# Rotary embedding moved into the projection's PSUM slot, with the statistics factor folded into its tables

## The reference

```python
def rms_norm(x, g):
    y = xf * lax.rsqrt(jnp.mean(xf * xf, axis=-1, keepdims=True) + NORM_EPS)
    return (y * g.astype(jnp.float32)).astype(x.dtype)

def partial_rope(x, cos, sin):
    x1, x2 = x[..., :half], x[..., half:2 * half]
    return concatenate([x1 * c - x2 * s, x2 * c + x1 * s, x[..., 2 * half:]], axis=-1)

h = rms_norm(x, norm_g)
q, k, v, gate = jnp.split(h @ w_in, 4, axis=-1)
q = partial_rope(q.reshape(B, L, 2 * A_HEADS, A_HEAD_DIM), cos, sin)
k = partial_rope(k.reshape(B, L, 2 * A_HEADS, A_HEAD_DIM), cos, sin)
...
w = p[:, :, 0] - lam * p[:, :, 1]          # two softmaxes of one head
```

## Time and profile before

| | us |
|---|---|
| Median of three runs | 3052.21 |
| The profiled execution | 3053.24 |
| Its span (first to last instruction) | 3051.5 |
| PE busy | 2915.2 |
| DVE busy | 1403.8 |
| POOL busy | 1225.6 |
| ACT busy | 979.3 |

### The profile page before, as it was taken

How to read it: one execution, slowest core, us unless ns; L and a number is a source line. 1 busy time by engine, 2 the same in 40 slices (tenths; PEclk the granted TensorE clock), 3 DMA queues, 4 the chain that set the end, 5 groups by cost and what they waited for, 6 DMA issues and landing times.

```text
span 3051.5 us, 41339 instructions
## 1 busy us (share of the span) xinstructions
PE 2915.2 (96%) x16960; PEld 2473.9 (81%) x16960; DVE 1403.8 (46%) x2243; ACT 979.3 (32%) x1440; POOL 1225.6 (40%) x888
## 2 busy tenths in 40 slices
PE   7999999999999988999999997999999999999976
PEld 7999999999899987777878786777777777777754
DVE  6443443434443448454444457432323334463556
ACT  4313222222313244334142434432232322333332
POOL 4343433434343423442534354544434343344331
PEclk9999999999999999999999998999999999999999
DMA  4121212222121212121212232322222222221211
GB/s 168 61 92 70 83 70 84 71 83 83 56 97 69 84 63 69 70 83 70 85 68 97 70 117 86 108 80 86 83 69 90 76 83 76 77 87 69 83 56 69
DMA packets 36944, 247.45 MB, mean 81 GB/s; under 512 B 3970, under 2 KB 4115, under 8 KB 8212
## 3 DMA queue, kind: packets, MB, share of 16 engines
q1 hardware_dynamic: 35728, 241.36, 22.4%
q10 hardware_dynamic: 1028, 3.44, 0.3%
HBM read 240.59 MB, written 4.19 MB: 80 GB/s over the span
## 4 chain that ended last, share of the span: by engine, by line
PE 85%; DVE 9%; ACT 2%; DVEq 2%; issue 1%; DMA 0%; ACTq 0%; POOL 0%; SPq 0%
PE pj L288 19%; PE pj L292 18%; PE pj L294 18%; PE pj L319 4%; PE pj L323 4%; PE pj L321 4%; PE pj L973 2%; PE pj L974 2%; PE pj L975 2%; DVE xl L366 2%; DVE arena L412 2%; PE pa L510 1%; PE pa L472 1%; PE pa L904 1%; DVEq L414 1%
## 5 line engine op out<-in xcount | busy, mean ns | idle before, releaser
L2041 POOL TENSOR_TENSOR wl<-raw,wh 128x512 fp32r<-128x512 f32 x884 | 1225.4, 1418 | 1790.6 <-ACT wh L264 1790.6
L288 PE MATMUL pj<-xh,wh 128*128 128x264 f32 (+2 forms) x3792 | 1112.6, 340 | 22.0 <-POOL wl L2041 17.7
L292 PE MATMUL pj<-xl,wh 128*128 128x264 f32 (+2 forms) x3792 | 1079.5, 331 | 13.4 <-DVE xl L366 13.3
L294 PE MATMUL pj<-xh,wl 128*128 128x264 f32 (+2 forms) x3792 | 1074.7, 330 | 0.0
L264 ACT ACTIVATE wh<-raw 128x2048 fp32r<-128x2048 f32 x221 | 423.0, 1914 | 1056.0 <-PE pj L294 647.7
L288 PEld LDWEIGHTS pj<-xh,wh 128*128 128x128 f32 x3792 | 651.1, 191 | 108.3 <-issue 41.1
L292 PEld LDWEIGHTS pj<-xl,wh 128*128 128x128 f32 x3792 | 648.9, 190 | 87.3 <-DVE xl L366 21.3
L294 PEld LDWEIGHTS pj<-xh,wl 128*128 128x128 f32 x3792 | 650.1, 191 | 64.8
L337 DVE TENSOR_TENSOR arena<-pj,rstd 128x512 f32<-128x512 f32 (+1 forms) x151 | 105.4, 698 | 399.1 <-PE pj L294 387.6
L319 PE MATMUL pj<-oh,wh 128*128 128x264 f32 (+1 forms) x800 | 222.7, 330 | 14.9 <-DVE ol L739 11.4
L345 DVE TENSOR_TENSOR acc<-pj,acc 128x528 f32<-128x528 f32 (+1 forms) x224 | 156.5, 699 | 143.4 <-PE pj L323 142.5
(11 more groups left out here) (276 smaller groups left out, 2657.2 us busy)
## 6 DMA issues: line engine op xcount, KB each, us to landing
raw<-in_stream SPq DMA_DIRECT2D x221, 1024.0 KB, 4.8
acc<-in_x SPq DMA_DIRECT2D x8, 528.0 KB, 9.2
out_y<-acc SPq DMA_DIRECT2D x8, 512.0 KB, 2.9
arena<-in_mem ACTq DMA_DIRECT2D x2, 1024.0 KB, 6.3
cst<-in_cst SPq DMA_DIRECT2D x1, 448.0 KB, 13.5
cos<-in_cos_a SPq DMA_DIRECT2D x1, 264.0 KB, 13.7
sin<-in_sin_a SPq DMA_DIRECT2D x1, 264.0 KB, 13.9
cos<-in_cos_b ACTq DMA_DIRECT2D x1, 264.0 KB, 2.8
```

The source lines that it names most:

```text
L288: pe.matmul(pj[:, pu, b, 0:m], whk, xh[:, k, a:a + m], start=(k == 0), stop=False)
L292: pe.matmul(pj[:, pu, b, 0:m], whk, xl[:, k, a:a + m], start=False, stop=False)
L294: ins = pe.matmul(pj[:, pu, b, 0:m], wlk, xh[:, k, a:a + m], start=False, stop=(k == KD - 1))
L2041: pool.tensor_tensor(wl[:, j, at], raw[:, j, at], wh[:, j, at].bitcast(F32), ALU.subtract).then_inc(s_part if c < LO_PARTS - 1 else s_lo, 1)
```

## The change

The statistics factor is multiplied into both tables once per layer (`fold_rstd`, two DVE instructions over 128 partitions). The rotary step reads the projection's PSUM slot: the product with the cosine table goes to SBUF, then the slot's rotated rows are shuffled in place (two instructions, one for each bank of 264), multiplied by the sine table in place, and added to the SBUF rows. The slot is handed back to PE after the last of these. For query 0 of the next head the shuffle goes from the slot to `tmp`, the slot is handed back after it, and one product with the sine table stands before add 4; the other steps inside `add_out` are gone. On PE the scores of units 0 and 1 stand ahead of k steps 5 and 8 instead of 3 and 7.

```diff
-            proj(pe, t + 2, u + 2, 0, 0, T, hooks={3: [a_scores(h, 0)], 7: [a_scores(h, 1)], 10: [a_scores(h, 2)],
+            proj(pe, t + 2, u + 2, 0, 0, T, hooks={5: [a_scores(h, 0)], 8: [a_scores(h, 1)], 10: [a_scores(h, 2)],
                                                    12: [a_wtr(h, 0, 0)], 15: [a_scores(h, 3)]})
-        def rope(dve, x, n, rows, mask):
-
-            dve.stream_shuffle(tmp[0:rows, 0:n], x[0:rows, 0:n], mask)
-            dve.drain()
-            dve.tensor_tensor(tmp[0:rows, 0:n], tmp[0:rows, 0:n], sin[0:rows, 0:n], ALU.mult)
-            dve.tensor_tensor(x[0:rows, 0:n], x[0:rows, 0:n], cos[0:rows, 0:n], ALU.mult)
-            dve.drain()
-            return dve.tensor_tensor(x[0:rows, 0:n], x[0:rows, 0:n], tmp[0:rows, 0:n], ALU.add)
...
+        def fold_rstd(dve, n):
+
+            for table in (cos, sin):
+                dve.tensor_tensor(table[:, 0:n], table[:, 0:n], rstd[:, 0:n], ALU.mult)
+            dve.drain()
+
+        def rope(dve, x, u, pu, n, rows, mask, view=None):
+
+            view = (lambda ap: tok(ap, n)) if view is None else view
+            ps = ps_out(pu, n)
+            dve.wait_ge(s_out, u + 2)
+            dve.tensor_tensor(x, view(ps) if n != T else ps, view(cos[:, 0:n]), ALU.mult)
+            dve.drain()
+            for b, at, m in halves(n):
+                half = pj[0:rows, pu, b, 0:m]
+                dve.stream_shuffle(half, half, mask)
+            dve.drain()
+            dve.tensor_tensor(ps[0:rows], ps[0:rows], tok(sin[0:rows, 0:n], n), ALU.mult)
+            dve.drain()
+            ins = dve.tensor_tensor(x[0:rows], view(ps[0:rows]) if n != T else ps[0:rows], x[0:rows], ALU.add)
+            dve.drain()
+            dve.sem_inc(s_evac, 1)
+            return ins
...
-            evac_scaled(dve, A_q[0], u + 1, 1, T).then_inc(s_evac, 1)
-            dve.drain()
-            steps = rope_steps(dve, A_q[0], T, A_ROT, A_MASK)
...
-                add_out(dve, w, T, 0, between={4: steps[0], 7: steps[1], 10: steps[2]})
...
+                dve.wait_ge(s_out, u + 3)
+                dve.tensor_tensor(tok(A_q[0], T), ps_out(1, T), tok(cos[:, :], T), ALU.mult)
+                for b, at, m in halves(T):
+                    dve.stream_shuffle(tmp[0:A_ROT, at:at + m], pj[0:A_ROT, 1, b, 0:m], A_MASK)
+                dve.drain()
+                dve.sem_inc(s_evac, 1)
+                x, y = A_q[0][0:A_ROT, :], tmp[0:A_ROT, :]
+                add_out(dve, w, T, 0, between={4: lambda: dve.tensor_tensor(y, y, sin[0:A_ROT, :], ALU.mult)})
+                dve.tensor_tensor(x, x, y, ALU.add)
+                dve.drain()
...
             dve.wait_ge(s_tab, 32)
+            fold_rstd(dve, T)
             for c in range(2):
-                evac_scaled(dve, B_x, U_KV + c, c, T).then_inc(s_evac, 1)
-                dve.drain()
-                rope(dve, B_x, T, P, B_MASK)
-                dve.drain()
+                rope(dve, tok(B_x, T), U_KV + c, c, T, P, B_MASK)
...
+            rope(dve, B_q[:, :, m, :], u, pu, SEQ, P, B_MASK, view=b_tok)
+            dve.sem_inc(s_bq, 1)
```

More of the change, by code:

```diff
@@ L646, in a_first @@
         def a_first(dve, u, w=None):
-            evac_scaled(dve, A_k[0], u, 0, T).then_inc(s_evac, 1)
-            dve.drain()
-            rope(dve, A_k[0], T, A_ROT, A_MASK).then_inc(s_rope, 1)
-            dve.drain()
-            evac_scaled(dve, A_q[0], u + 1, 1, T).then_inc(s_evac, 1)
-            dve.drain()
-            steps = rope_steps(dve, A_q[0], T, A_ROT, A_MASK)
+            rope(dve, tok(A_k[0], T), u, 0, T, A_ROT, A_MASK)
+            dve.sem_inc(s_rope, 1)
             if w is None:
-                for f in steps:
-                    f()
-            else:
-                add_out(dve, w, T, 0, between={4: steps[0], 7: steps[1], 10: steps[2]})
-            dve.drain()
-            dve.tensor_tensor(A_q[0][0:A_ROT, :], A_q[0][0:A_ROT, :], tmp[0:A_ROT, :], ALU.add).then_inc(s_rope, 1)
-            dve.drain()
+                rope(dve, tok(A_q[0], T), u + 1, 1, T, A_ROT, A_MASK)
+            else:
+                dve.wait_ge(s_out, u + 3)
[8 more added lines that the diff above has]
+                dve.drain()
+            dve.sem_inc(s_rope, 1)
         def a_dve(dve, h, last=False):
@@ L666, in a_dve @@
             for j, x in enumerate([A_k[1], A_q[1]]):
[L667 to L670, removed]
+                rope(dve, tok(x, T), u + j, j, T, A_ROT, A_MASK)
+                dve.sem_inc(s_rope, 1)
             for j in (2, 3, 4):
```

## The result

The changed kernel takes 3035.67 us (median of 5 runs, 3035.24 to 3041.51) beside 3052.28 of the kernel before in the same comparison: ratio 0.9945, 95% interval 0.9931 to 0.996, so 12 to 21 us faster. In a second comparison it was 3038.19 beside 3055.42, ratio 0.9946 (0.9933 to 0.996). The profiled execution took 3035.24 us, its span is 3033.5, against 3053.24 and 3051.5 before.

A forecast was written before the change was run, and what follows sets the result against it. PE was taken to bound the kernel, so only its waits counted; the terms summed to -6.6 us, from the profiled 3053.24 to 3046.6, or 3045.6 at the runs' median, with a range of 3040.0 to 3052.0.

The forecast's parts named there:

- (a): First layer's heads: PE's wait at unit 1's scores goes, 1.93 us a head in 8 heads, -15.4 us.
- (b): First layer's heads: a new wait at unit 2's scores for unit 1's exponential, 0.27 us times 8, +2.1 us.
- (c): Second output of w_out: PE waits for query 0's slot, 0.6 us in each of 7 heads, +4.2 us.
- (d): Steps between w_out's adds: the old cosine step before add 10 goes, -0.31 us in 7 heads, -2.2 us.
- (f): Shared keys: slot freed later, PE waits 3.4 us and loses 1.7 to the lower clock, together +5.1 us.
- (e): First layer's start: table products and longer slot hold delay PE by +4.2 us, with no change for the clock.
- R: Duration of the new rotary step on DVE, forecast at 3.4 us against 5.8 before.
- (g): Second layer: the 1.04 us wait at a group's first scores goes, with restart, in 4 groups, -4.6 us.
- its rival: First rival: cheap slots, no clock loss at the shared keys; -11.6 us, 3040.6 us, chance 0.13.
- the fourth rival: SBUF slowness is not POOL's, so the new add stays slow; -1.2 us, 3051.0; chance 0.20 together with the second rival.

The follow-up runs named there:

- places only: The kernel before with only the scores of units 0 and 1 moved, to k steps 5 and 8; 3043.77 us, ratio 0.9962.
- unit 1 later: The kernel before, old rotary step, with unit 1 ahead of k step 9, unit 2 of 12, first transposes of 13; 3039.67 us, ratio 0.9951.
- wait filled: The kernel before with 14 extra, unneeded matmuls ahead of unit 1's scores in each head; 3046.81 us, ratio 0.9977.
- second layer only: The kernel before with the new rotary form for the second layer's queries alone; 3048.76 us, ratio 0.998.

## Why the prediction was wrong, point by point

- **(a) the scores' wait, -15.4.** Its mechanism and its 1.93 us a head hold: -1.93 + 0.1 (b) + 0.38 (c) - 0.31 (d) = -1.76, the measured period is 1.75 shorter. The step failed in that it priced the wait by its length alone, read in head 0. Two of the seven periods of that trace were 138.7 us instead of 137.1. In (f) the prediction had itself read what a gap does to the clock, and did not put the same question to eight gaps of 1.66 us. This term, put at nothing, was 3.2 us in the trace, 4 on average.
- **(b) unit 2, +2.1:** measured 0.1 us in 8 heads, +0.8. DVE saw unit 1 0.6 us after its start, not 0.7, since unit 1 no longer started behind a wait.
- **(c) query 0's slot, +4.2:** 0.38 x 7 = +2.7. The shuffle pair took 0.81 us (168.21 to 169.02) and began 0.08 before the product's end; from its end to PE's start were 0.08 us, where I had put 0.2 for drain, semaphore and PE.
- **(d) -2.2:** nothing speaks against it; the sine product at add 4 took 0.83 and delayed nothing.
- **(e) start, +4.2:** PE starts 3.6 us later (52.88 against 49.27), since R was 3.15 and not 3.4. Nothing was put for the clock; it stayed at its lower level for 6.1 us behind the start instead of 4.7, +0.6. The second pair of traces has +2.8 for the whole start.
- **(f) shared keys, +5.1; (g) second layer, -4.6:** together +0.5 forecast and +0.5 measured. (g) alone is -4.8 by its own experiment. In (f) PE stood still for 3.56 us, and the clock behind it was granted at 0.66 over 5 us, 1.7 us lost, as forecast; in front of it the clock had risen earlier than before, which gave 0.4 back: 4.8.
- The terms' sum, rightly sized, is -9.4 us, 2.8 more than forecast, from (b) and (c). With 4 us of clock in the heads it is 13.4, inside the measured 12 to 21. From the three runs' 3052.2, the named terms alone would end at 3042.8, inside the range; with the clock they end at 3038.8, below it. The medians of the two comparisons differ by 16.6 and 17.2 us, so 3 to 4 us more stay open. The range failed because its low end was made of the bounds of the named terms alone, and no rival let the clock be better in the heads than in the trace.
- **Slips in the sums.** The range begins at 3040.0 where its rival was worked out as 3040.6, and the fourth rival's terms add up to -1.1 rather than -1.2. Neither decides anything.
- **The starting point.** The three runs lay 3 us or more below the medians of the 50 later runs beside which the experiments stood. Three runs did not show that spread. Medians of one code also differ: 11 more runs of the kernel before had 3049.84 beside 3055.45 in the same comparison (ratio 0.9982 to 1.0003, so no difference is shown). Five of the kernels here (the changed one, places only, unit 1 later, wait filled, second layer only) lie 0.6 to 5.5 us further below before's median than the parts named for them add up to. Since one code's medians differed by 5.6 us, a remainder of this size proves nothing.

**What stays open.** Behind the second layer, in unchanged code, the first pair of traces differs by 4.3 us. The two traces of before take 1177.6 and 1181.6 there, the two after 1173.2 and 1176.3; over all thirteen traces it is 1173 to 1182. Equal waits with unequal clocks are there too: two of 2.04 us, in before

```profile
2503.50:2507.50 4.00, 4.00 (x14) 3.23 (x15) 0.00 (x0) 0.60 (x1) 3.96 (x4) 0.65 0.01 4
2612.10:2616.10 4.00, 3.98 (x20) 3.34 (x21) 0.00 (x0) 0.60 (x1) 4.00 (x4) 1.00 0.00 0
```

At the same two places after, the clock was 1.00 behind the first and 0.61 behind the second: they have changed roles. What made the difference in the first pair were, above all, two more falls of the clock in before, at 2781 and 2819 us (1.2 and 1.7 us lost), and a wait for ACT at L1723 of 2.30 us that was 0.92 after. The seven traces with the old step in the first layer take 1178.5 us behind the second layer on average (1174.7 to 1181.6), the six with the new one 1175.6 (1173.2 to 1178.4). The two overlap, and two of the seven have neither of these falls; whether the change shortens this part, or chance did in these traces, is not shown.

## What to carry to other kernels

Where TensorE is the bound, ask of each of its waits first what other work could stand in front of it: moving three hooks gave nearly as much as the new rotary step did with its slow starts (15.8 and 17.2 us by the medians; with quick starts the new step came to 31.7). A wait costs more than its length when the clock falls behind it, and it falls behind some of several equal waits only; cut the trace into periods that should be equal and look for the long ones. A slot may be held longer only where the engine that frees it is early; at a stage's start, where it waits for a statistic, read the first output in the shortest way and do everything else behind it.

## What the runs showed of the hardware that was not expected

- Behind equal waits of TensorE of 1.66 to 1.69 us the granted clock fell in 10 of 32 heads (four traces), to 0.64 over the next 4.5 us; in each trace the fallen heads stood three apart. Behind waits of 0.93 to 0.95 us it fell in none of 8, and with the wait filled in none of 8. Behind the two later waits of 2.04 us it fell in 14 of 26 (thirteen traces).
- DVE worked in place on PSUM as fast as elsewhere: a shuffle of 264 columns took 0.42 to 0.44 us, a product of 528 with input and output in PSUM 0.70.
- A DVE product with both inputs in SBUF took 0.71 us alone and 1.78 beside POOL's; with one input in PSUM it was 0.71 in both cases. Over all 528-column products and adds in the trace of before: with both inputs in SBUF, 0.69 to 0.71 us in the 76 with no POOL instruction beside them, 1.64 in the median of the 89 mostly beside one; with an input in PSUM, 0.69 to 0.71 in all 196. POOL gained as well: 1.37 us a part instead of 1.42.
